# Norm gain moved into the weight tiles, and the last weight columns in six deeper tiles, in a two-block transformer kernel

## What is computed

```python
h = _rmsnorm(x, norm_mix_pre[l]).astype(dt)   # x * rsqrt(mean(x*x) + eps) * g
z = h @ w_in[l]                                # 1024 x 3084 weights
z_a, z_b, z_c, z_d = _split(z, GROUP_SPLITS)   # four mixers: rwkv, mlstm, window, fox
```

## Time and profile before

| what | value |
|---|---|
| median of 3 runs | 3032.17 us |
| the profiled execution's own time | 3030.39 us |
| its span (first to last instruction) | 3028.6 us |
| TensorE busy | 2713.7 us, 90% |
| VectorE busy | 2083.4 us, 69% |
| ScalarE busy | 1377.5 us, 45% |
| GpSimd busy | 594.2 us, 20% |

### The profile page before, as it was taken

How to read it: one execution, slowest core, us unless ns; L and a number is a source line. 1 busy time by engine, 2 the same in 40 slices (tenths; PEclk the granted TensorE clock), 3 DMA queues, 4 the chain that set the end, 5 groups by cost and what they waited for, 6 DMA issues and landing times. The chain is left out here.

```text
span 3028.6 us, 41801 instructions
## 1 busy us (share of the span) xinstructions
PE 2713.7 (90%) x14251; PEld 2258.0 (75%) x14251; DVE 2083.4 (69%) x2645; ACT 1377.5 (45%) x2180; POOL 594.2 (20%) x386
## 2 busy tenths in 40 slices
PE   7999996899969999998599997867887799999998
PEld 7787775777858888887577786656776688887886
DVE  6995517765479999998535355666664888887677
ACT  5122417632258888887432213466344333332544
POOL 1232212620012111110222120101100533331000
PEclk9999998999979999999799998888998899999999
DMA  3112219643179999998522221041114123332734
GB/s 114 38 47 84 80 66 306 222 153 134 56 303 416 415 413 415 413 416 326 188 56 66 71 74 43 3 125 29 29 63 153 28 84 84 84 84 75 245 104 158
DMA packets 269374, 474.18 MB, mean 157 GB/s; under 512 B 35285, under 2 KB 154244, under 8 KB 269220
## 3 DMA queue, kind: packets, MB, share of 16 engines
q1 hardware_dynamic: 240676, 405.48, 37.9%
q10 hardware_dynamic: 19696, 36.71, 3.3%
q0 software_dynamic: 8848, 29.96, 3.0%
HBM read 379.73 MB, written 92.35 MB: 156 GB/s over the span
## 5 line engine op out<-in xcount | busy, mean ns | idle before, releaser
L2255 DVE TENSOR_TENSOR e_w_lo<-e_ring,e_w_hi 128x1024 fp32r<-128x1024 f32 x384 | 446.9, 1220 | 46.1 <-ACT e_w_hi L2182 46.1
L2182 ACT CAST e_w_hi<-e_ring 128x1024 fp32r<-128x1024 f32 x384 | 377.2, 1048 | 35.2 <-PE banks L2115 28.6
L2113 PE MATMUL banks<-e_w_hi,e_xT_hi 128*128 128x512 f32 x512 | 202.7, 396 | 0.0
L2115 PE MATMUL banks<-e_w_hi,e_xT_lo 128*128 128x512 f32 x512 | 199.9, 391 | 0.0
L2114 PE MATMUL banks<-e_w_lo,e_xT_hi 128*128 128x512 f32 x512 | 199.6, 390 | 0.0
L1065 DVE SCALAR_TENSOR_TENSOR conv<-x_first,vectors,conv 128x1024 f32<-128x1024 f32 x120 | 185.5, 1546 | 9.8 <-issue 0.9
L1039 POOL TENSOR_TENSOR p_w_lo<-p_w,p_w_hi 128x1024 fp32r<-128x1024 f32 (+1 forms) x48 | 107.2, 2235 | 323.7 <-ACT p_w_hi L963 314.4
L2991 PE MATMUL banks<-u_sums,u_w_hi 128*128 128x512 f32 (+1 forms) x364 | 140.1, 385 | 11.0 <-DVE u_sums L3170 9.6
L2056 POOL COPY e_pick<-expert_index 128x1 int32 x31 | 64.8, 2089 | 416.4 <-PE banks L2106 405.8
L895 PE MATMUL banks<-h_hi,p_w_hi 128*128 128x512 f32 x352 | 141.2, 401 | 0.9 <-POOL p_w_lo L1039 0.9
L2992 PE MATMUL banks<-u_sums,u_w_hi 128*128 128x512 f32 (+1 forms) x364 | 139.8, 384 | 0.0
(11 more groups left out here) (661 smaller groups left out, 7447.1 us busy)
## 6 DMA issues: line engine op xcount, KB each, us to landing
e_ring<-in_w_gate_e_dram SPq DMA_DIRECT2D x128, 512.0 KB, 6.3
e_ring<-in_w_up_e_dram SPq DMA_DIRECT2D x128, 512.0 KB, 6.5
e_ring<-in_w_down_e_dram SPq DMA_DIRECT2D x128, 512.0 KB, 5.4
u_w<-in_ffn_w_up_dram SPq DMA_DIRECT2D x44, 512.0 KB, 5.8
expert_results<-nothing SPq DMA_DIRECT2D x1, 16384.0 KB
expert_results<-e_y ACTq DMA_DIRECT2D x32, 512.0 KB, 7.6
p_w<-in_w_in_dram SPq DMA_DIRECT2D x24, 512.0 KB, 3.6
t_raw<-in_ffn_w_down_dram SPq DMA_DIRECT2D x11, 1024.0 KB, 7.4
```

Source lines behind the costliest of these rows:

```text
L2113: mm(bank, xT_hi[:, b, k, :], w_hi[:, part, cols], start=(k == 0), stop=False)
L2115: last = mm(bank, xT_lo[:, b, k, :], w_hi[:, part, cols], start=False, stop=(k == KT - 1))
L2182: nc.scalar.copy(w_hi[:, part, :], experts.ring[:, slot, :]).then_inc(w_rounded, 1)
L2255: tt(w_lo[:, part, :], experts.ring[:, slot, :], w_hi[:, part, :].bitcast(F32), ALU.subtract).then_inc(w_split, 1)
```

## The change

The gain leaves the norm. ScalarE rounds a transposed tile right from the bank, and VectorE subtracts from the bank; `whole` is gone. Each weight tile is multiplied by the gain, broadcast over columns, before it is rounded: tiles 0 and 1 by VectorE ahead of its splits, all others by GpSimd. GpSimd multiplies tiles 2 and 3 behind its gathers, and tile n + 2 right behind the split of tile n; it now waits for the loads, and ScalarE's `fill` waits for the multiply. Squares are taken tile by tile, `mean` of the first pair comes ahead of the third add. A slab's tile has the full 1024 elements a partition: feature blocks by columns, 2 x 512 or 4 x 256, so 16 tiles become 6 (n = 20 to 25). For a tile TensorE does all feature blocks of one token tile before the next token tile. The score stores move to n = 19 and the reload to n = 20. Storing the inverse and the wait for it go from ScalarE to SP, behind SP's last weight load.

```diff
-class CombinedNorm(PairNorm):
+class CombinedNorm(RowNorm):
...
+    def bank(self, t):
+        return self.K.ps[:, 4 + 2 * (t % 2):6 + 2 * (t % 2), :].rearrange("p c (k n) -> p (c k) n", n=P)
+
+    def turn(self, pe, t):
+        pe.wait_ge(self.scaled, t + 1)
+        if t >= 2:
+            pe.wait_ge(self.parted, t - 1)
...
+    def round_off(self, act, t):
+        act.wait_ge(self.turned, t + 1)
+        self.K.nc.scalar.activation(self.hi[:, :, t * P:(t + 1) * P], self.bank(t), ACT.Copy).then_inc(self.rounded, 1)
+
+    def rest(self, dve, t):
+        tokens = slice(t * P, (t + 1) * P)
+        dve.wait_ge(self.rounded, t + 1)
+        self.K.nc.vector.tensor_tensor(self.lo[:, :, tokens], self.bank(t), self.hi[:, :, tokens].bitcast(F32),
+                                       ALU.subtract).then_inc(self.parted, 1)
...
     def on_scalar(self, act):
...
         self.square(act, 0)
+        self.square(act, 1)
         self.root(act, 0)
         act.wait_ge(self.rated, 1)
         self.scale(act, 0)
         self.scale(act, 1)
-        self.square(act, 1)
+        self.square(act, 2)
         for q in range(PAIRS):
             self.round_off(act, 2 * q)
             if q + 1 < PAIRS:
-                self.root(act, q + 1)
+                self.square(act, 2 * q + 3)
             self.round_off(act, 2 * q + 1)
             if q + 1 < PAIRS:
+                self.root(act, q + 1)
                 act.wait_ge(self.rated, q + 2)
                 self.scale(act, 2 * q + 2)
                 self.scale(act, 2 * q + 3)
             if q + 2 < PAIRS:
-                self.square(act, q + 2)
+                self.square(act, 2 * q + 4)
...
     def on_vector(self, dve):
         self.add(dve, 0)
         self.add(dve, 1)
-        self.add(dve, 2)
         self.mean(dve, 0)
         self.rate(dve, 0)
+        self.add(dve, 2)
         self.add(dve, 3)
         for q in range(PAIRS):
             t = 2 * q
-            self.times_gain(dve, t)
-            self.times_gain(dve, t + 1)
+            self.rest(dve, t)
             if q + 1 < PAIRS:
                 self.mean(dve, q + 1)
-            self.rest(dve, t)
+            self.rest(dve, t + 1)
             if q + 1 < PAIRS:
                 self.rate(dve, q + 1)
-            self.rest(dve, t + 1)
...
+    depths = [KT * P // m for m in widths]
+    chunks = [(s, c) for s, depth in enumerate(depths) for c in range(KT // depth)]
...
+        def with_gain(n):
+            ks, tile = tiles(n)
+            return tile, norm.gain[:, ks].unsqueeze(2).to_broadcast(list(tile.shape))
...
                 sp.wait_ge(split, n - 1)
+                ks, tile = tiles(n)
                 for col, m, at in pieces:
...
+                    sp.dma_start(tile[:, :, at:at + m], w_in[:, ks, col:col + m], allow_slow_non_contiguous=True).then_inc(landed[n % 2], 16)
+            if beside:
+                beside.on_sync(sp)
...
+            for n, (s, c) in enumerate(chunks, U):
+                m, depth, b = widths[s], depths[s], n % 2
+                pe.wait_ge(split, n + 1)
+                for t in range(NT):
+                    if c == 0:
+                        pe.wait_ge(kept, done if s == 0 else done + (s - 1) * NT + t + 1)
+                    bank, tokens = K.ps[:, t, 0:m], slice(t * P, (t + 1) * P)
+                    for i in range(depth):
+                        k, cols = c * depth + i, slice(i * m, (i + 1) * m)
+                        mm(bank, h_hi[:, k, tokens], w_hi[:, b, cols], start=(k == 0), stop=False)
...
             def fill(n):
...
-                if n >= 2:
-                    loads[n % 2] += 16 * len(pieces_of[n])
-                    act.wait_ge(landed[n % 2], loads[n % 2])
-                nc.scalar.activation(w_hi[:, n % 2, 0:sizes[n]], w[:, n % 2, 0:sizes[n]], ACT.Copy).then_inc(rounded, 1)
+                act.wait_ge(w_gained, n + 1)
+                nc.scalar.activation(w_hi[:, n % 2], w[:, n % 2], ACT.Copy).then_inc(rounded, 1)
...
+            times_gain(2)
+            times_gain(3)
+            for n in range(2, U + C):
                 pool.wait_ge(rounded, n + 1)
...
                     .then_inc(split, 1)
+                if n + 2 < U + C:
+                    times_gain(n + 2)
...
         def _(dve):
+            for n in range(2):
+                tile, gain = with_gain(n)
+                nc.vector.tensor_tensor(tile, tile, gain, ALU.mult).then_inc(w_gained, 1)
...
-        if n == 21:
+        if n == 19:
             act.wait_ge(self.cut, NT)
...
-        if n == 22:
+        if n == 20:
             act.wait_ge(self.m_saved, 16 * 8)
             act.dma_start(self.rows[:], self.scratch["minus"]).then_inc(self.m_loaded, 16)
-        if n == 34:
-            act.wait_ge(self.solved, 1)
-            act.dma_start(self.scratch["inverse"], self.inverse()).then_inc(self.t_saved, 16)
-        if n == 35:
-            act.wait_ge(self.t_saved, 16)
+
+    def on_sync(self, sp):
+        sp.wait_ge(self.solved, 1)
+        sp.dma_start(self.scratch["inverse"], self.inverse()).then_inc(self.t_saved, 16)
+        sp.wait_ge(self.t_saved, 16)
```

More of the change, by code:

```diff
@@ L576, in on_sync, with square, root, on_scalar @@
             sp.dma_start(self.keep[t * P:(t + 1) * P, :], self.x[:, t, :]).then_inc(self.x_kept, 16)
-    def square(self, act, q):
-        for t in (2 * q, 2 * q + 1):
-            act.wait_ge(self.added, t + 1)
-            self.K.nc.scalar.activation(self.junk, self.x[:, t, :], ACT.Square, accum_out=self.rstd[:, t:t + 1])
-            act.drain()
-        act.sem_inc(self.squared, 1)
-    def on_scalar(self, act, between={}):
+    def square(self, act, t):
+        act.wait_ge(self.added, t + 1)
+        self.K.nc.scalar.activation(self.junk, self.x[:, t, :], ACT.Square, accum_out=self.rstd[:, t:t + 1])
+        act.drain()
+        act.sem_inc(self.squared, 1)
+    def root(self, act, q):
+        pair = self.rstd[:, 2 * q:2 * q + 2]
+        act.wait_ge(self.meaned, q + 1)
+        self.K.nc.scalar.activation(pair, pair, ACT.Sqrt).then_inc(self.rooted, 1)
+    def on_scalar(self, act):
         PAIRS = NT // 2
@@ L616, in add, with mean, rate @@
         last.then_inc(self.added, 1)
+    def mean(self, dve, q):
+        pair = self.rstd[:, 2 * q:2 * q + 2]
+        dve.wait_ge(self.squared, 2 * q + 2)
+        self.K.nc.vector.tensor_scalar(pair, pair, 1.0 / D, EPS, ALU.mult, ALU.add).then_inc(self.meaned, 1)
+    def rate(self, dve, q):
+        pair = self.rstd[:, 2 * q:2 * q + 2]
+        dve.wait_ge(self.rooted, q + 1)
+        self.K.nc.vector.reciprocal(pair, pair).then_inc(self.rated, 1)
     def on_vector(self, dve):
@@ L660, in project_columns, with tiles @@
         stage = K.sb(scope, f"{tag}_stage", [P, SLOTS, HALF]) if stores else None
-        sizes = [KT * P] * U + [m for m in widths for _ in range(KT)]
-        pieces_of = [pieces for pieces, *_ in units] + [pieces for pieces, _ in slabs for _ in range(KT)]
+        pieces_of = [pieces for pieces, *_ in units] + [slabs[s][0] for s, _ in chunks]
+        def tiles(n):
+            if n < U:
+                return slice(0, KT), w[:, n % 2].rearrange("p (k n) -> p k n", k=KT)
+            s, c = chunks[n - U]
+            return slice(c * depths[s], (c + 1) * depths[s]), w[:, n % 2].rearrange("p (k n) -> p k n", k=depths[s])
+        def with_gain(n):
+            ks, tile = tiles(n)
+            return tile, norm.gain[:, ks].unsqueeze(2).to_broadcast(list(tile.shape))
         @block.sync
@@ L701, in _ @@
                 beside.leave_banks(pe)
[L702 to L716 removed]
+            for n, (s, c) in enumerate(chunks, U):
[8 more added lines that the diff above has]
+                        mm(bank, h_hi[:, k, tokens], w_hi[:, b, cols], start=(k == 0), stop=False)
+                        mm(bank, h_hi[:, k, tokens], w_lo[:, b, cols], start=False, stop=False)
+                        last = mm(bank, h_lo[:, k, tokens], w_hi[:, b, cols], start=False, stop=(k == KT - 1))
+                    if t == NT - 1:
+                        last.then_inc(chunked, 1)
+                    elif k == KT - 1:
+                        last.then_inc(projected, 1)
         @block.scalar
@@ L771, in _ @@
                     beside.on_scalar(act, u)
-            for s, (_, out) in enumerate(slabs):
-                for k in range(KT):
-                    n = s * KT + k
-                    if k < KT - 1:
-                        act.wait_ge(chunked, n + 1)
-                        fill(U + n + 2)
-                    if beside:
-                        beside.on_scalar(act, U + n)
+            for n, (s, c) in enumerate(chunks, U):
+                if c < KT // depths[s] - 1:
+                    act.wait_ge(chunked, n - U + 1)
+                    fill(n + 2)
+                if beside:
+                    beside.on_scalar(act, n)
+                if c < KT // depths[s] - 1:
+                    continue
+                out = slabs[s][1]
                 for t in range(NT):
@@ L4384, in mixers @@
```

(1 more changed line is left out.)

60 lines of the change are left out of this document (23 added, 37 removed).

## The result

The changed kernel takes **3012.95 us** (median of six, 3006.97 to 3019.94); the kernel before, run beside it, 3032.15 (six, 3028.8 to 3037.66). The ratio is 0.9936 with an interval of 0.9922 to 0.995: faster, by 19.2 us. The forecast was 3017.7, its range 3013.0 to 3023.0. The direction was right, and so were the three places where the changed stage gains; the gain of the whole was 4.7 us larger than the sum, because the block behind the stage, taken as unchanged, became about 4 us shorter. The median stands 0.05 us under the range. The profiled execution of the changed kernel took 3015.02 us, with a span of 3013.2, 1.8 less, as before.

A forecast was written before the change was run, and what follows sets the result against it. The prediction took TensorE's finish and the barrier's slowest other engine as the bound. Norm 5.0, slabs 4.0 and barrier 5.5 sum to 14.5 us, taking the median of 3032.17 to 3017.7, range 3013 to 3023.

The forecast's parts named there:

- What bounds it: Changed stage: TensorE waits for VectorE in the norm, is full in units and slabs, idles 9.64 us at the barrier.
- The norm: Norm up to unit 2: gain multiplies leave VectorE, fourth pair of token tiles released 5.0 us earlier; bounds -2.4 and -5.9.
- the gathers' term: Start of the norm: VectorE's added multiplies make the gathers start 0.45 us late, between 0 and 0.7.
- Weight tiles 0 and 1: VectorE ahead of its splits: two added multiplies, 2.4 us, covered by its idle time.
- GpSimd's multiplies: Units and slabs: 24 multiplies of 2.4 us, hidden in a 9.1 us cycle under TensorE's 10.9; cost zero, bounds 0 to 2.
- rival C: Units and slabs: GpSimd becomes the bound with a cycle of 14.0 us, kernel slower at 3058 us; chance 0.04.
- Slabs: Slab stretch: 16 tiles become 6, no bank late, 66.9 us against 70.9, so -4.0; bounds 0 and -4.0.
- The tail: Barrier after the slabs: TensorE's idle 4.1 us in place of 9.64, so -5.5; bounds -4.5 and -6.0.
- Behind the barrier: Block after the barrier: shifts unchanged, with 0 to -1 us if the clock stays at its upper level longer.
- A: Norm doesn't speed up, gathers slip beside GpSimd's multiplies: -2 to -3 in place of -5, about 3020.5 us; chance 0.13.
- D: Whole kernel: gains given back in the clock after the barrier or in late tiles, no change, 3029 us; chance 0.05.
- rival B: Barrier stays held by SP's store of the inverse or a late solve: only 9 of 14.5 us come, 3023; chance 0.08.

The follow-up runs named there:

- no_multiply: Changed kernel without GpSimd's multiplies of weight tiles 2 to 25 by the gain: 3013.58 us, ratio 0.9941 to the kernel before.
- gain_only: Changed kernel with one feature block a slab tile and the tail of before, keeping new norm and multiplies: 3036.03 us, ratio 1.0009 to the kernel before.
- before_again: The kernel before, unchanged, profiled a second time: 3035.82 us in one execution.
- before_third: The kernel before, unchanged, profiled a third time: 3033.38 us in one execution.
- block_order: Changed kernel, but each feature block of a slab tile passes all eight banks in turn, as before: 3016.74 us, ratio 0.9952 to the kernel before.
- late_scores: Changed kernel with the score stores at n = 20, one slab tile later, reload right behind them: 3013.70 us, ratio 0.9943 to the kernel before.
- inverse_scalar: Changed kernel with the inverse's store and wait back on ScalarE at n = 24 and 25: 3016.20 us, ratio 0.9949 to the kernel before.
- tail_before: Changed kernel with score stores one slab tile later and the inverse's store and wait back on ScalarE: 3021.35 us, ratio 0.9959 to the kernel before.
- slabs_only: Changed kernel with the norm of before and no weight tile multiplied, keeping deep slab tiles and new tail: 3023.28 us, ratio 0.9964 to the kernel before.

## Why the prediction was right, and where it was wrong

*What bounds it* was right in each part: the same three places changed, and no new wait of TensorE came up. The sum of the stage, -14.5, met the -14.7 at equal clocks, but partly by luck: the norm gained 1.2 more than its term, the tail 0.6 more and the slabs 1.6 less.

*The norm* was under-sized: -6.24 for -5.0, past the bound of -5.9. Its bound was "if the gathers are not late at all" (by the step's own 0.45 us that gives -5.45, and -5.9 has no working), and they were not: the first gather starts at 1458.92, 1.56 us after the block's first work at 1457.36, and the issues took the same 1.61 and 0.94, 1.9 us apart, as in the earlier trace rows, although VectorE now had four instructions there and not two. The first pair comes 23.93 us after the first gather, where the forecast has 1478.9 - 1454.20 = 24.70 and the kernel before 25.18: 0.77 us, of which the gathers' term is 0.45. The pairs took 27.17 for 27.6, another 0.4; the walk itself was right, down to the last pair bounded by TensorE. So the 1.61, which the step read as a leak from VectorE's work, did not grow with it.

*Weight tiles 0 and 1*: covered, as said. *GpSimd's multiplies*: they cost TensorE nothing, shown by no_multiply, and VectorE's solve 2.2 us. One takes 1.90 us alone and not the 2.4 taken; the mean of the 24 is 2.04, that of the splits 2.70. The cycle at its tightest was 8.8 us for 9.1. Of rival C nothing was seen in deep tiles, but gain_only shows that its mechanism is real where tiles are small. The Trainium skill (GPSIMD Engine Reference, section 4.1) has GpSimd about twice as slow as VectorE for two inputs. The split agrees, 2.37 against 1.2; the multiply, with its gain broadcast over columns, does a little better, 1.90 against VectorE's 1.18 for tiles 0 and 1.

*Slabs*: -4.03 for -4.0, and the match is luck. The step took the stretch at 0.67 for a part of the kernel; before_again and before_third don't have it, and the tiles give 2.4. *The tail*: -6.07 for -5.5, since the barrier opened 2.8 us behind the last store in place of 3.2, and that store was issued sooner than estimated. block_order, late_scores, inverse_scalar and tail_before show each part. The step had the reasons right but not how they join: the early scores are worth 0.3 us while the store is on SyncE, and 11.47 - 4.98 = 6.5 if it weren't.

*The step that failed* is "Behind the barrier everything shifts as it is. TensorE's shorter idle may leave the clock at its upper level a little longer: 0 to -1". The block behind the barrier took 4.1 us less in the two profiles, and in the repeats 133.8 against 139.1 and 136.4; it ran at a granted clock of 0.87 in place of 0.84, with the same work. The idle, which the step named, is not its cause, and the cause stays open. By the means of all profiles of the two kernels the stage is 14.7 us shorter and the block behind it 4.1; that makes 18.8, and the medians differ by 19.2. (The first two profiled executions are only 15.4 apart: the first gather of the one after came 4.7 us later, 1458.92 for 1454.20, in code that the change does not touch.) The low end of the range, 3013.0, had only 1 us for the clock and nothing for the scatter of the executions. A block at a mean granted clock of 0.84 can give or take several us, and one window of TensorE over it would have shown that before: the low end belonged some 3 us lower.

Rivals A and D did not occur. Of rival B one half did: GpSimd's longer instructions took 4.8 us of the solve's lead, 39.9 us becoming 44.7, where B needed all 9; the barrier wasn't held. Its other half, a barrier held by the inverse, is tail_before.

## What to carry to other kernels

Before an operation is put into a loader's chain of two buffers, compare its cycle (load, operation, split) with what the consumer needs for the smallest tile, not for the typical one: here 5 us against 2.9 ate the whole gain, and deeper tiles, 11 us of work each, gave it back. Two moves in the tail of a stage can each look worthless when undone alone (0.3 and 1.4 us) and be worth 7.9 together, so undo pairs as well as single edits, and check whether the tail that comes back is the one you started from. And where the next stage runs at a varying granted clock, read it in several executions before its difference is put to the change, and leave room for it in the range.

## What was not expected of the hardware

**GpSimd and VectorE took turns.** The earlier trace rows had GpSimd's split stretched from 2.37 to 4.11 us beside a product of VectorE. In the kernel after VectorE's products are stretched as well; its timeline beside the multiply and the split shown above:

```profile
1670.99 2.28 DVE L4020 TENSOR_TENSOR rwkv_kk<-rwkv_kk,z_rwkv 128x2048 f32<-128x2048 f32 x1
1673.20 3.98 DVE L4021 TENSOR_TENSOR x_first<-x_first,z_rwkv 128x2048 f32<-128x2048 f32 x1
1677.11 4.47 DVE L4022 TENSOR_TENSOR x_first<-x_first,z_rwkv 128x2048 f32<-128x2048 f32 x1
```

In each case the instruction that starts second grows by about what is left of the other's. VectorE's first product begins 0.34 us before GpSimd's multiply and keeps its 2.28; the multiply, with 1.94 us of it to go, takes 3.71 in place of 1.90. The second product begins with 1.84 of the multiply to go and takes 3.98, the split with 1.35 of that product to go takes 3.61, and the third product with 2.33 of the split to go takes 4.47. Small instructions pay most for their size: the solve's product of 128x121 above, 0.28 us of work, began 0.04 us behind the split and ended 0.15 us after it. VectorE's sums of one tensor in the solve were not touched, 15.7 us for all 31 in every kernel. The Trainium skill (GPSIMD Engine Reference, section 1) names such contention for VectorE instructions with two SBUF inputs; the trace agrees, and adds that either side may be the one that waits. TensorE was not held up by any of it.

**Spells at the lower level may repeat or not.** slabs_only gave the same spells of the lower level in two executions, to 0.1 us over 138; gain_only gave 134.5 and 139.05 for one program. The Trainium skill (TensorE: Matmul & The Clock Gate, Part 1) has the clock follow how busy the array has lately been. The program is the same in both executions of gain_only, so by the trace that rule alone does not foretell the length of this block to better than 4.6 us.
